# The first four modulation pieces go from VectorE sums to TensorE products in four 32-column tiles; x is loaded first, small vectors from GpSimd's queue

## The reference: one conditioned decoder layer over 512 tokens

```python
c_act = jax.nn.silu(c)                                    # (1, 1024)
mod = (c_act @ ada_w[l] + ada_b[l])[:, None, :]           # 1024 x 6144
sh_a, sc_a, gt_a, sh_f, sc_f, gt_f = jnp.split(mod, 6, axis=-1)
h = rmsnorm(x, norm_mix_g[l]) * (1.0 + sc_a) + sh_a
proj = h @ w_in[l]                                        # 512 x 2320
...                                                       # two token mixers
mix = jnp.concatenate([o_gla, o_swa], axis=-1) @ w_out[l]
x = x + gt_a * mix
h = rmsnorm(x, norm_ffn_g[l]) * (1.0 + sc_f) + sh_f
y = hier_moe(h, w_grp, b_grp, w_exp, b_exp, w_gate, w_up, w_down)
x = x + gt_f * y
return rmsnorm(x, final_norm_g)
```

## Time and profile before

| what | us |
|---|---|
| median of 3 runs (583.42, 588.17, 588.43) | 588.17 |
| profiled execution, span from first to last instruction | 591.2 |
| PE busy in that span | 512.2 (87%) |
| DVE busy | 284.6 (48%) |
| ACT busy | 147.1 (25%) |
| first transposes of x on PE begin | 23.22 |
| first projection begins | 29.46 |
| product of piece 4 (`("mod", 4)`) begins | 59.22 |

### The profile page before, as it was taken

The page is one execution under the profiler, slowest core; times in us unless marked ns, Lnnn a source line. Parts: engine busy times, 40 slices in busy tenths (PEclk is TensorE's granted clock), DMA queues, the critical chain, the costliest instruction groups (busy, mean ns, idle before and its releaser), DMA issues.

```text
span 591.2 us, 7201 instructions
## 1 busy us (share of the span) xinstructions
PE 512.2 (87%) x2644; PEld 292.3 (49%) x2644; DVE 284.6 (48%) x700; ACT 147.1 (25%) x370; POOL 80.2 (14%) x128
## 2 busy tenths in 40 slices
PE   0497999999999998999983999999888987797981
PEld 0353585545656565455653555555444544344430
DVE  4589817484747473555554256323112321123275
ACT  2502214142434270222030312222111321120221
POOL 5000000000100000001122222222122221111101
PEclk9989889979999999999995899999889998798996
DMA  8999962950970005691017999999999999999673
GB/s 292 377 346 277 343 250 81 386 178 0 267 302 2 1 1 213 257 369 60 25 71 253 357 395 398 414 414 407 399 414 417 387 415 418 391 388 420 257 303 142
DMA packets 57981, 163.88 MB, mean 277 GB/s; under 512 B 10339, under 2 KB 13940, under 8 KB 51034
## 3 DMA queue, kind: packets, MB, share of 16 engines
q1 hardware_dynamic: 46632, 147.95, 66.0%
q0 software_dynamic: 6192, 12.38, 5.6%
q10 hardware_dynamic: 5122, 3.08, 1.8%
HBM read 155.48 MB, written 16.58 MB: 291 GB/s over the span
## 4 chain that ended last, share of the span: by engine, by line
PE 63%; DMA 14%; SPq 13%; DVE 3%; issue 3%; ACT 1%; ACTq 1%; POOL 1%; POOLq 0%; DVEq 0%
PE ps L1572 22%; PE ps L1840 10%; PE ps L1751 9%; DMA early<-in_w_up 6%; SPq L498 5%; PE ps L1853 4%; SPq L502 3%; DMA wide<-in_w_up 2%; SPq L504 2%; DMA xres<-in_x 2%; DMA wide<-y_rows 2%; PE ps L1829 2%; ACTq L772 1%; PE ps L1777 1%; PE ps L1617 1%
## 5 line engine op out<-in xcount | busy, mean ns | idle before, releaser
L1572 PE MATMUL ps<-ring,hreg 128*128 128x512 f32 (+1 forms) x320 | 136.6, 584 | 2.1 <-DVE hreg L1053 2.1
L1572 PEld LDWEIGHTS ps<-ring,hreg 128*128 128x128 f32 x320 | 63.5, 203 | 65.5 <-issue 60.0
L1440 DVE TENSOR_TENSOR turned<-turned,ps 64x256 f32<-64x256 f32 x33 | 14.0, 423 | 135.5 <-ACT turned L949 135.5
L1840 PE MATMUL ps<-ring,proj 128*64 128x256 f32 x288 | 70.6, 401 | 7.8 <-DMA ring<-in_w_up 7.2
L1841 PE MATMUL ps<-ring,proj 128*64 128x256 f32 x288 | 70.6, 401 | 0.0
L1840 PEld LDWEIGHTS ps<-ring,proj 128*64 128x64 f32 x288 | 40.2, 144 | 31.0 <-DMA ring<-in_w_up 7.6
L1024 DVE SCALAR_TENSOR_TENSOR wide<-wide,csil 128x512 f32<-128x512 f32 x72 | 49.1, 746 | 2.5 <-DMA wide<-in_ada_w 2.5
L949 ACT ACTIVATE turned<-ps 64x256 f32<-64x256 f32 x33 | 12.4, 375 | 143.7 <-PE ps L1841 143.7
L701 POOL DMA_INDIRECT y_rows<-proj,hreg x31 | 30.9, 997 | 109.8 <-DVE proj L1446 109.8
L643 POOL TENSOR_TENSOR rstd<-ssq,halfm 128x1 f32<-128x1 f32 (+1 forms) x13 | 10.0, 766 | 232.6 <-DVE ssq L1323 140.5
L1841 PEld LDWEIGHTS ps<-ring,proj 128*64 128x64 f32 x288 | 40.3, 145 | 0.0
(11 more groups left out here) (331 smaller groups left out, 792.7 us busy)
## 6 DMA issues: line engine op xcount, KB each, us to landing
wide<-in_ada_w SPq DMA_DIRECT2D x24, 1024.0 KB, 8.7
ring<-in_w_gate SPq DMA_DIRECT2D x17, 1024.0 KB
ring<-in_w_up SPq DMA_DIRECT2D x17, 1024.0 KB
ring<-in_w_down SPq DMA_DIRECT2D x17, 1024.0 KB, 23.5
wide<-in_w_down SPq DMA_DIRECT2D x10, 1024.0 KB
ring<-in_w_in SPq DMA_DIRECT2D x4, 2048.0 KB, 9.6
proj<-in_w_gate SPq DMA_DIRECT2D x5, 1024.0 KB
proj<-in_w_up SPq DMA_DIRECT2D x5, 1024.0 KB
```

Of the source, the lines that this page charges most:

```text
L1572: mm = pe.matmul(ps[bank_of(st)][:, 0:CW[ch]], hT[:, k, b * P:(b + 1) * P], win_sb[ch][:, k, :], start=k == 0, stop=k == KD - 1)
L1840: pe.matmul(ps[bank][0:TILE, 0:F], hx[k], w_cols(w, 0, k), start=k == 0, stop=k == KD - 1)
```

## The change: pieces 0 to 3 on PE

`csilp` holds silu(c) as the first of 32 columns for each k, the rest zeros. Each half piece is now multiplied by four products of 32 output rows, one for each of its k, each into another 32-partition strip of one PSUM bank (`piece_rows`). The second half accumulates onto the first. DVE copies the bank to `acc` (`keep_rows`), and `sum_columns` goes on as before. The bias rows and the gain come as a 24x128 block, transposed once on PE and copied by DVE to `vcol`. DVE adds them where it read the columns out of bank 7.

Two more buffers, in `proj`, let five half pieces be in flight. x is issued ahead of piece 0. Chunk 0 of `w_in` is loaded in two halves. The nine small loads go from ACT to POOL, behind the second pair's column vectors. The order on PE is rewritten. Pieces 4 to 11 are as before. The semaphores of x's copy at the end (`y_in`) are shared with others, with larger counts.

```diff
+ON_PE = 4
+ADA_SLOT = [0, 1, 2, 3, 4, 0, 1, 2] + [q % 3 for q in range(2 * ON_PE, 2 * NPC)]
+ROW_BANK = [0, 1, 3, 6]
...
+            for i, rows in enumerate((norm_mix_g[0:1, :], ada_b[0:1, PARTS[0] * D:(PARTS[0] + 1) * D],
+                                      ada_b[0:1, PARTS[1] * D:(PARTS[1] + 1) * D])):
+                sp.dma_start(vrow[i * KD:(i + 1) * KD, :], rows.rearrange("l (k p) -> (l k) p", p=P)).then_inc(vrow_in, 16)
...
+                    if ada_uses(q) > 1:
+                        before = max(a for a in range(q) if ADA_SLOT[a] == slot)
+                        if before < 2 * ON_PE:
+                            sp.wait_ge(ada_used, before + 1)
+                        else:
+                            sp.wait_ge(ada_rows, KH * (before - 2 * ON_PE + 1))
...
-            piece(0)
             for b in range(NB):
                 sp.dma_start(xres[:, b, :], x_v[b]).then_inc(x_in[b], 16)
+            piece(0)
             piece(2)
-            win(0)
+            first_win(0)
             piece(1)
             piece(3)
+            first_win(1)
             win(1)
...
+            def few(o, i):
+                pool.dma_start(o, i).then_inc(small_in, 16)
+            pool.wait_ge(col_vec, 2)
...
-                act.dma_start(mcol[:, 2, :], norm_mix_g.rearrange("l (k p) -> p (l k)", p=P)).then_inc(gain_in, 16)
...
+            def keep_rows(i):
+
+                n = FIRST.index(i)
+                dve.wait_ge(ada_used, 2 * (n + 1))
+                if n >= 2:
+                    dve.wait_ge(mod_col, n - 1)
+                dve.tensor_copy(acc[:, n % 2, :], ps[ROW_BANK[n]][:, :]).then_inc(acc_ready, 1)
 
-            piece(0)
+            dve.wait_ge(ada_used, 1)
+            dve.tensor_copy(vcol[:, :, :], ps[2][:, 0:3 * KD].rearrange("p (a k) -> p a k", a=3)).then_inc(cols_ready, 1)
             dve.wait_ge(ssq_ready, NB)
             dve.tensor_scalar(ssq[:, 0:NB], ssq[:, 0:NB], 1.0 / D, EPS, ALU.mult, ALU.add).then_inc(mean1_ready, 1)
...
+            def piece_rows(i):
+
+                n = FIRST.index(i)
+                for kh in range(2):
+                    q = 2 * n + kh
+                    slot = ADA_SLOT[q]
+                    pe.wait_ge(ada_sem[slot], 16 * ada_uses(q))
+                    for j in range(KH):
+                        mm = pe.matmul(ps[ROW_BANK[n]][32 * j:32 * (j + 1), :], csilp[:, kh * KH + j, :],
+                                       (ada_sb + ada_more)[slot][:, j, :], start=kh == 0, stop=kh == 1)
+                    mm.then_inc(ada_used, 1)
+
+            pe.wait_ge(vrow_in, 3 * 16)
+            pe.transpose(ps[2][:, 0:3 * KD], vrow, ident[0:3 * KD, 0:3 * KD])
+            pe.wait_ge(cols_ready, 1)
+            piece_rows(0)
             pe.wait_ge(xs_ready, NB)
             for k in range(4):
                 turn_x(k)
+            sum_columns(0)
+            piece_rows(2)
             sum_columns(2)
...
+            project(("proj", 0, 0), range(4))
+            project(("proj", 0, 1), range(4))
+            for k in range(4, 6):
                 turn_x(k)
+            piece_rows(1)
+            project(("proj", 0, 2), range(4))
+            piece_rows(3)
             sum_columns(1)
+            project(("proj", 0, NB - 1), range(4))
             sum_columns(3)
-            project(("proj", 0, NB - 1), range(4))
+            turn_x(6)
             pe.wait_ge(h_dve, 3)
             turn_x(7)
             pe.wait_ge(h_dve, 4)
             pe.wait_ge(h_act, 3)
+            pe.wait_ge(win_in0b, 16)
             project(("proj", 0, 0), range(4, 7))
```

More of the change, by code:

```diff
@@ L169, in layer_kernel @@
         pflat = proj[:, :, :].rearrange("p b n -> p (b n)")
+        ada_more = [proj[:, 0:KH, D + i * PC:D + (i + 1) * PC] for i in range(2)]
         scm = proj[:, :, 0:D]
@@ L317, in layer_kernel @@
         ov_free = sem('ov_free')
[L319 to L322, removed]
+        fg_in, y1_added, y2_added, y_squared = (
+            sem(n) for n in ('fg_in', 'y1_added', 'y2_added', 'y_squared'))
         y_mean, y_rstd, ynorm, out_done = (
@@ L644, in _ @@
             power(0, 4, mean1_ready, 1, rstd1_ready)
+            def few(o, i):
+                pool.dma_start(o, i).then_inc(small_in, 16)
+            pool.wait_ge(col_vec, 2)
+            with nc.allow_non_contiguous_dma("broadcast loads of small vectors"):
+                few(sinks[:, :], swa_sinks[0:1, :].broadcast_to([P, SH]))
+                few(gla_g[:, :], gla_norm_g.rearrange("l h v -> l (h v)").broadcast_to([P, GH * DV]))
+                few(wa2[0:RANK, :], gla_w_a2[0])
+                few(wa2[RANK:RANK + 1, :], gla_b_a2)
+                few(fcol[:, 2, :], norm_ffn_g.rearrange("l (p k) -> p (l k)", k=KD))
+                few(wr[:, :, 0:NG], w_grp.rearrange("l (p k) n -> p (l k) n", k=KD))
+                few(wr[:, :, NG:], w_exp.rearrange("l (p k) n -> p (l k) n", k=KD))
+                few(br[:, 0:NG], b_grp[0:1, :].broadcast_to([P, NG]))
+                few(br[:, NG:], b_exp[0:1, :].broadcast_to([P, NE]))
             pool.wait_ge(turn_ready, TURN[("proj", 1, NB - 1)] + 1)
@@ L769, in _ @@
             act.activation(csil[:, :], ccol[:, :], ACT.Exp, scale=-1.0).then_inc(silu_e, 1)
-            def few(o, i):
-                act.dma_start(o, i).then_inc(small_in, 16)
-            with nc.allow_non_contiguous_dma("column and broadcast loads of small vectors"):
+            with nc.allow_non_contiguous_dma("column loads of a small vector"):
                 act.dma_start(posi[:, :], positions.rearrange("a (b p) -> p (a b)", p=P)).then_inc(pos_in, 16)
-                act.dma_start(mcol[:, 2, :], norm_mix_g.rearrange("l (k p) -> p (l k)", p=P)).then_inc(gain_in, 16)
             for b in range(NB):
@@ L789, in _ @@
                                bias=mcol[:, 1, k:k + 1]).then_inc(h_act, 1)
[L791 to L798, removed]
-                few(br[:, 0:NG], b_grp[0:1, :].broadcast_to([P, NG]))
-                few(br[:, NG:], b_exp[0:1, :].broadcast_to([P, NE]))
             act.wait_ge(ang_ready, 1)
@@ L1005, in piece @@
                 a = acc[:, n % 2, :]
+                r0 = KD * (n - ON_PE)
                 if i >= 6:
@@ L1037, in _ @@
             for half in range(2):
-                if half == 0:
-                    piece(2)
-                    dve.wait_ge(gain_in, 16)
-                else:
-                    piece(1)
-                    piece(3)
+                keep_rows(FIRST[2 * half])
+                keep_rows(FIRST[2 * half + 1])
                 cols = slice(4 * half, 4 * half + 4)
+                dve.wait_ge(cols_ready, 2)
                 dve.wait_ge(mod_col, 2 * half + 2)
-                link(dve.tensor_copy(mcol[:, 0:2, cols],
-                                     ps[7][:, 0:2 * KD].rearrange("p (a k) -> p a k", a=2)[:, :, cols]))
-                dve.scalar_tensor_tensor(out=mcol[:, 3, cols], in0=mcol[:, 0, cols], scalar=1.0, in1=mcol[:, 2, cols],
+                link(dve.tensor_tensor(mcol[:, 0:2, cols],
+                                       ps[7][:, 0:2 * KD].rearrange("p (a k) -> p a k", a=2)[:, :, cols],
+                                       vcol[:, 1:3, cols], ALU.add))
+                dve.scalar_tensor_tensor(out=mcol[:, 3, cols], in0=mcol[:, 0, cols], scalar=1.0, in1=vcol[:, 0, cols],
                                          op0=ALU.add, op1=ALU.mult).then_inc(col_vec, 1)
```

65 lines of the change are left out of this document (39 added, 26 removed).

## The result

The changed kernel takes 595.9 us (median of 595.22 to 599.68), the kernel before in the same call 588.3: a ratio of 1.0165 with a 95% interval of 1.0113 to 1.0217. A second measurement gave 595.16 against 587.28, 1.015 with 1.0094 to 1.0206. So it is slower by more than 1% (the second interval reaches down to 0.94%), which had a chance of 0.28; 592.1 was forecast, with 586 to 598 as the range.

The account below looks back on a forecast made before the run. TensorE's chain was taken to bound the kernel, a shift of the product of piece 4 shifting the end one for one: +5.8 for its delay, -1.9 for a vanished low clock stretch, +3.9 in sum: 592.1 us, range 586 to 598.

Parts of the forecast that it names:

- Loads: Front loads: x at 11.5, piece 0's first half at 14.2, piece 2 at 22.7; nothing later than 14.2 waited for.
- The wait that the change adds: Means of x stand behind a copy awaiting the first half piece's product: means 16.4, transposes 22.1, a gain of 1.1.
- Up to the first projection: Transposes, column sums and piece 2 in a row on TensorE, 1.9 a piece: first projection at 32.1, 2.6 later.
- rival 3: Products of piece rows: tiles do not overlap four at a time; with two, +11.0 in all, 599; chance 0.10.
- To the end of the second pair: TensorE from first projection through pieces 1 and 3 to the last column sum: 22.2, ending at 54.3; hT 56.3.
- What is late next: Product of piece 4: VectorE's angle chain and piece 4 behind hT put it at 65.0, not 59.22: +5.8, wait 1.7.
- After it: Behind the product of piece 4: shorter wait, busy TensorE, so the clock stays up: -1.9, sum +3.9.
- rival 1: At the wait for the product of piece 4 the clock falls after all: +5.8, 594; chance 0.18.
- Small loads: Nine loads on GpSimd start at 54.8, issued by 66, in by 84: no wait at `decay_logit`, 11 us to spare.
- Rival 4: Small loads late if GpSimd cannot issue during VectorE's sums of pieces 4 to 7: +14 to +20, some 605; chance 0.05.
- Rival 2: Clock stays up in the front, perhaps also at 84: up to -2.5, 585.7; chance 0.15 shared with rival 5.
- rival 5: Piece 2's landing decides: first projection at 27.5, sum -0.7, 587.5; chance 0.15 shared with Rival 2.

Follow-up runs that it names:

- small loads alone: Kernel before with only the nine small loads moved from ScalarE's queue to GpSimd's: 583.35 us against 589.62, ratio 0.994.
- pieces 1 and 3 back on VectorE: Changed kernel with VectorE's means and angle chain moved earlier, and only pieces 0 and 2 on TensorE: 580.47 us, ratio 0.9904 to the kernel before.
- means first: Changed kernel with VectorE's means of x ahead of the copy of the bias and gain columns: 590.54 us, ratio 1.0048 to the kernel before.
- x first alone: Kernel before with only the four loads of x issued ahead of piece 0's: 587.79 us, ratio 1.0025.
- the filled wait: Changed kernel with two unread 512-column products added on TensorE ahead of the product of piece 4: 593.45 us, ratio 1.0106 to the kernel before.
- angles early: Changed kernel with VectorE's angle chain ahead of the second pair's copies: 595.57 us, ratio 1.012 to the kernel before.
- both together: Changed kernel with the means ahead of the `vcol` copy and the angle chain right behind it: 587.9 us against 588.42 for the kernel before.

## Why the prediction was wrong, point by point

- **Loads, right.** First half piece used at 14.47 (forecast 14.2); piece 2 had landed by its turn. Of the later landings TensorE waited only for the second half of piece 0, 0.69 us at 17.09, while x was still being normalised, at no cost.
- **The wait that the change adds, right.** Means at 16.56 (16.4), transposes at 22.27 (22.1). Taking the wait away brought the product of piece 4 forward by 3.1 us.
- **Up to the first projection, right.** 32.34 (32.1). A piece takes 1.92, so four tiles overlap almost wholly and rival 3 falls. The Trainium skill, "TensorE: Matmul & The Clock Gate", Part 3, has 3.07 times for four row tiles; sixteen passes one after the other would be 6.87, so here, for four column tiles, it is 6.87/1.92 = 3.6. The measurement decides.
- **To the end of the second pair, right.** Last column sum ends at 54.48 (54.3), hT at 56.51 (56.3). That pieces 1 and 3 were hidden on VectorE and cost TensorE's path 5.3 there is what the run with both back on VectorE shows.
- **"Apart from the sum of piece 2": not so.** In one place the prediction excepts that sum from what was hidden before, in another it has it end while TensorE transposed. The second is right: in the kernel before its last step ends at 26.26, and TensorE goes from the transposes (to 26.5) to the column sum without a wait.

```profile
25.57 0.69 DVE L1031 TENSOR_TENSOR wide<-wide 128x512 f32<-128x512 f32 x1
```

All four sums were hidden, this one with half a microsecond to spare at most in the three profiles. What set the front was x: in the chain of waits its landing (16.30), the means (17.50) and the scaling (to 23.18) stand ahead of the transposes.

- **What is late next, right in kind and 0.8 short.** 65.77 (65.0), behind VectorE with a wait of 2.07 (1.7). Half of that is the 1.27 us of piece 4's first two products, 0.88 in the kernel before, which lie beside a GpSimd issue (see below).
- **After it: the step that failed.** It took the low stretch at the product of piece 4 for a fixed cost of the old wait, 1.9 us, and booked its going as a gain since the new wait is shorter. All three profiles of the changed kernel have that stretch, with the sign that the prediction names for rival 1 (0.18): a granted clock near 0.50 behind the product. Two of three of the kernel before have none, behind 3.75 and 3.87 us of idling; against them there was nothing to take away. The sum at `decay_logit` should have read +6.0 for the order and then, against an execution of the kernel before without stretches, +4.4 for two of them. Without the 1.9 the prediction's own sum gives rival 1's 594. That 595.9 lies inside the range is luck: its upper end, 598, was put there for tiles that overlap by half, which did not come.
- **The base.** The difference was worked out in a profile 3.0 above the median and added to the median. That profile holds both stretches, the executions at 585 and 586 us hold neither. Of 19, 35 and 11 runs of the kernel before the medians were 589.62, 588.42 and 587.28, the extremes 581 and 593, so the size of the loss depends on which of its executions one meets: 2.3 in the span against the first profile, 9.6 against the others, 7.6 and 7.9 by medians.
- **A shift of the product of piece 4 as a shift of the end, one for one: not quite.** Of 6.1 us at the gather against the first profile 3.8 came back behind it, of 11.9 against the others 2.2.
- **Small loads, right.** Nine issues from 55.26 to 61.13, 0.65 each and not 1.24; `decay_logit` has no wait. Rival 4 falls (an issue was held up in three other runs, but by 0.2 us, see below). Rival 2 falls with the granted clock of 0.50 at the first projection, rival 5 with its start at 32.34.

By its parts, the way of the product of piece 4 from 59.46 (before, second profile) to 65.77 is: the small loads off ScalarE, -3.3 (to 56.17); pieces 1 and 3 on TensorE, +5.3; the means behind the copy, +3.1; the angle chain and piece 4 behind a later hT, +1.7 (62.68 to 60.95); and -0.5 (56.17 to 55.63) between the small loads alone and pieces 1 and 3 back on VectorE. Of that last part 0.37 us is the wait on VectorE, whose angle chain is out of the way. The first projection begins at 29.70 in the one and at 29.78 in the other, so x first with pieces 0 and 2 on TensorE won nothing there. The parts add up to +6.3; they are differences of single profiles.

What stays open is what decides that an execution draws a low stretch. The runs show only where it came: behind 2.07 us of waiting in four of four profiles with that wait (the changed kernel's three and the one with means first), behind 3.7 to 3.9 in one of three, and behind 3.18 in the one profile of x first alone, a long execution. Four of the ten executions with means first took 585.9 to 587.5 us with a mean clock of 0.950 to 0.952, where the profiled one has 0.944, so they may lack a stretch; no profile shows it.

## What to carry to other kernels

Before moving a sum to another engine, look at whether it was on the path: here none of the four was, and two of them cost 5.3 us on the engine that bounds the kernel. In a queue that runs in order, a copy that waits for a product should not stand ahead of work that is ready. And a stretch of low clock in one profile is no fixed price: take a second profile before a sum counts on its going.

## What the runs showed of the hardware

Four tiles of 32 columns, 512 columns of moving data each in fp32, ran almost wholly side by side: 16 passes in 1.92 us, against 0.43 for one.

GpSimd's issue of a load and a VectorE product from one input got in each other's way. Where piece 4's first two products begin while a `wr` issue runs they took 1.26 to 1.27 us (the changed kernel's three profiles, the small loads alone, the means first, the filled wait), elsewhere 0.87 to 0.88, and the two issues 0.93 and 0.89 either way. Where the products were running when the first `wa` issue began (angles early, both together, pieces 1 and 3 back on VectorE), they took 0.87 and the issue 0.75 in place of 0.54. The lines of "both together":

```profile
53.84 0.87 DVE L1054 TENSOR_SCALAR wide<-wide,csil 128x512 f32<-128x512 f32 x2
54.06 0.75 POOL L678 DMA_DIRECT2D wa<-in_gla_w_a  x1
```

The Trainium skill, "SBUF — State Buffer", "Who interferes with whom", says that between GpSimd and a VectorE instruction in a two-port mode the one that is first holds the shared ports and the other is blocked. These traces agree, if the plain products run in such a mode, which no trace shows: VectorE lost 0.4 us as the second, GpSimd 0.2. GpSimd's loss is what rival 4 feared, and it was small.

One kernel was seen with and without a low stretch at the same place behind the same wait, 4.0 to 4.4 us apart by `decay_logit`. And TensorE's first products in a front took 1.93 us for eight, in place of 1.05, while the granted clock in the row read 1.00 (14 to 16 us in the changed kernel). The records don't say why. So a granted clock of 1.00 in a row is not proof of the full rate: the time of a pass has to be read beside it.
